# Projections behind two layer ends made block by block, with the norm's transposes between their matmuls, and a third layer that opens with a quarter of z together with the dt columns

## What is computed

```
# layers A and B (A: latent attention, B: attention with forget gates)
hn = rms_norm(h, norm_pre[i])
proj = hn @ w_in[i]                       # values, queries, keys, gates, ...
y = concat(main, mem_out) * silu(gate)
h = h + rms_norm(y @ w_out[i], norm_post[i])
# layer C: a state space branch (SSD) and stick-breaking attention
h = rmsnorm(x, norm_pre)
z_ssd, xbc, dt_raw, q, k, v, z_sb, gates = split(h @ w_in)
xbc = silu(conv(xbc));  dt = softplus(dt_raw + dt_bias)
y = ssd_scan(xs, dt, -exp(a_log), bm, cm, d_skip)    # 16 heads
y_ssd = gated_group_rmsnorm(y, z_ssd) @ w_ssd_proj   # y * silu(z_ssd)
out = (g_ssd * y_ssd + g_sb * y_sb) @ w_out;  x + rmsnorm(out, norm_post)
```

## Time and profile before

| | |
|---|---|
| time, median of 3 | 1274.64 us (1274.6 to 1274.72) |
| time of the profiled execution | 1276.48 us |
| its span, first to last instruction | 1274.7 us |
| PE busy | 1233.7 us (97%) |
| ACT, DVE, POOL busy | 579.5, 530.1, 438.5 us |
| granted TensorE clock, mean | 0.997 |

### The profile page before, as it was taken

The page is one execution under the profiler, slowest core; times in us unless marked ns, Lnnn a source line. Parts: engine busy times, 40 slices in busy tenths (PEclk is TensorE's granted clock), DMA queues, the critical chain, the costliest instruction groups (busy, mean ns, idle before and its releaser), DMA issues. The chain is left out here.

```text
span 1274.7 us, 16603 instructions
## 1 busy us (share of the span) xinstructions
PE 1233.7 (97%) x6339; PEld 947.7 (74%) x6339; DVE 530.1 (42%) x983; ACT 579.5 (45%) x1215; POOL 438.5 (34%) x241
## 2 busy tenths in 40 slices
PE   8999989999999999999899999999999999999998
PEld 7988745578988666678677777778666667878786
DVE  4211655634210455452466445420577771021343
ACT  6354655644333655453544323263555653332242
POOL 5534301213344222213244554343322323444451
PEclk9999989999999999999999999999999999999999
DMA  7433201202235999612223112223211112322331
GB/s 280 133 99 65 66 14 46 67 18 67 79 105 91 72 80 92 84 48 85 67 83 100 50 50 77 72 83 98 68 51 50 51 50 84 98 91 92 99 99 67
DMA packets 111311, 101.01 MB, mean 79 GB/s; under 512 B 22068, under 2 KB 97152, under 8 KB 111232
## 3 DMA queue, kind: packets, MB, share of 16 engines
q1 hardware_dynamic: 108688, 95.35, 31.8%
q0 software_dynamic: 864, 3.15, 0.7%
q10 hardware_dynamic: 1680, 1.44, 0.4%
HBM read 94.68 MB, written 2.10 MB: 76 GB/s over the span
## 5 line engine op out<-in xcount | busy, mean ns | idle before, releaser
L480 POOL TENSOR_TENSOR w_lo<-w_raw,w_hi 128x1024 fp32r<-128x1024 f32 (+4 forms) x172 | 391.7, 2278 | 769.5 <-ACT w_hi L475 769.5
L475 ACT ACTIVATE w_hi<-w_raw 128x1024 fp32r<-128x1024 f32 (+4 forms) x172 | 171.3, 996 | 279.5 <-PE bank L531 237.6
L531 PE MATMUL bank<-acts_hi,w_hi 128*128 128x512 f32 (+1 forms) x600 | 231.8, 386 | 6.4 <-POOL w_lo L480 4.7
L531 PE MATMUL bank<-acts_lo,w_hi 128*128 128x512 f32 (+1 forms) x600 | 230.2, 384 | 0.0
L531 PE MATMUL bank<-acts_hi,w_lo 128*128 128x512 f32 (+1 forms) x600 | 230.2, 384 | 0.0
L531 PEld LDWEIGHTS bank<-acts_hi,w_hi 128*128 128x128 f32 x600 | 112.0, 187 | 32.5 <-issue 5.2
L531 PEld LDWEIGHTS bank<-acts_lo,w_hi 128*128 128x128 f32 x600 | 112.0, 187 | 23.1
L531 PEld LDWEIGHTS bank<-acts_hi,w_lo 128*128 128x128 f32 x600 | 112.0, 187 | 22.3
L531 PE MATMUL bank<-w_hi,acts_hi 128*128 128x512 f32 (+3 forms) x324 | 114.2, 353 | 4.0 <-POOL w_lo L480 1.7
L531 PE MATMUL bank<-w_hi,acts_lo 128*128 128x512 f32 (+3 forms) x324 | 113.5, 350 | 0.0
L531 PE MATMUL bank<-w_lo,acts_hi 128*128 128x512 f32 (+3 forms) x324 | 113.5, 350 | 0.0
(11 more groups left out here) (255 smaller groups left out, 2032.8 us busy)
## 6 DMA issues: line engine op xcount, KB each, us to landing
w_raw<-in_w_in SPq DMA_DIRECT2D x68, 512.0 KB, 3.6
w_raw<-in_w_out SPq DMA_DIRECT2D x24, 512.0 KB, 3.5
w_raw<-in_w_in_b SPq DMA_DIRECT2D x22, 512.0 KB, 4.8
w_raw<-in_w_in_a SPq DMA_DIRECT2D x10, 512.0 KB, 3.8
w_raw<-in_w_mem_kv SPq DMA_DIRECT2D x8, 512.0 KB, 8.0
w_raw<-in_w_sb_proj SPq DMA_DIRECT2D x8, 512.0 KB, 3.4
w_raw<-in_w_ssd_proj SPq DMA_DIRECT2D x8, 512.0 KB, 3.5
w_raw<-in_w_in_b SPq DMA_DIRECT2D x8, 384.0 KB, 3.1
```

The lines of the kernel that those rows point to most:

```text
L475: nc.scalar.activation(w_at(p)[0][:, 0:size], w_raw[p % RAW][:, 0:size], ACT.Copy).then_inc(w_high.sem, 1)
L480: nc.gpsimd.tensor_tensor(lo[:, 0:size], w_raw[p % RAW][:, 0:size], hi[:, 0:size].bitcast(F32), ALU.subtract).then_inc(w_rest.sem, 1)
L531: mm = nc.tensor.matmul(bank_of(S, s, g)[0:lhs.shape[1], 0:rhs.shape[1]], lhs, rhs, start=j + kk + t == 0, stop=j == len(S.pieces) - 1 and ...
```

## The change

Four things change.

1. `pB_v`'s first chunk goes block by block, and turns stand inside projections (`turns_in`): turn 0 after the first piece of block 2 of `pA_out`/`pB_out`, turn 1 after the first piece of its block 3, turns 2 and 3 inside blocks of the projection that follows. The `keep_busy` matmuls at both layer ends are gone. `out_act` rounds four or five pieces ahead instead of two.
2. Layer C opens with `pC_zd`: 256 columns of z and the 16 of dt as one projection of width 272, block by block, four pieces of two rows. `pC_dt` and its transposes are gone. Each of its pieces is fetched by two DMAs (`parts_in`).
3. What is left of z's first half is a chunk of 256 columns. `BESIDE` has more matmuls in slots 0 to 13, and the last slot has 66 instead of 110.
4. `w_more` grows (its start and end, `AR0` and `AR1`, move), two blocks of z stand in `row`, and POOL loads `norm_post` rows later: after all of `pB_v`'s pieces, and after the SSD gates.

```diff
-        pB_v = project(wb, 2 * MAIN_W, 384, 2, MB, tb, to_columns(b_v))
+        pB_v = project(wb, 2 * MAIN_W, 384, 2, MB, tb, to_columns(b_v), by_block=0)
...
-        pC_dt = project(wc, DT0, C_H, 1, 1, by_tokens, lambda S, k, s, g: dtT)
+        ZW = 256
+        pC_zd = project(wc, Z0, ZW + C_H, 1, MB, tb, lambda S, k, s, g: z_left[g][:, 0:ZW], by_block=0,
+                        parts=((Z0, ZW), (DT0, C_H)), rows_each=2)
...
-        pC_z = project(wc, Z0, 512, 2, MB, tb, None)
+        pC_z = project(wc, Z0 + ZW, 512 - ZW, 1, MB, tb, None, rows_each=2)
+        pC_zr = project(wc, Z0 + 512, 512, 1, MB, tb, None)
...
+                    if (block, j) in turns_in:
+                        norm_pe_step(pe, *turns_in[block, j])
...
             for m in range(MB):
                 square(0, m)
+            next_piece(0)
             post_root(0)
             pre_root(0)
             post_root(1)
             rows(0)
             pre_root(1)
             post_root(2)
-            next_piece(0, 4)
+            next_piece(1, 4)
             rows(1)
-            if ahead > 2:
-                next_piece(1, 5)
+            next_piece(2, 5)
             pre_root(2)
-            if ahead > 2:
-                next_piece(2, 6)
             post_root(3)
-            next_piece(*((3, 7) if ahead > 2 else (1, 7)))
+            next_piece(3, 7)
             rows(2)
+            next_piece(4, 6)
             pre_root(3)
             rows(3)
...
-        BESIDE = [3] * (2 * MB) + [4] * C_G + [5, 5] * (C_H + 1) + [6] * (4 * (MB - 1))
+        BESIDE = [6] * (2 * MB) + [8] * C_G + [9, 9, 9, 5] + [5, 5] * (C_H - 1) + [6] * (4 * (MB - 1))
...
-            project_pe(pe, pA_out, ready=attA.low, between_blocks=lambda g: end_blocks(pe, pre[1], g))
-            last_blocks(pe, pre[1], post[0])
-            project_pe(pe, pB_v, pre[1])
+            project_pe(pe, pA_out, ready=attA.low, turns_in={(2, 0): (pre[1], 0), (3, 0): (pre[1], 1)})
+            project_pe(pe, pB_v, pre[1], turns_in={(0, 1): (pre[1], 2), (1, 2): (pre[1], 3)})
...
+            project_pe(pe, pC_zd, pre[2], turns_in={(0, 1): (pre[2], 2), (2, 0): (pre[2], 3)})
+            project_pe(pe, pC_x, also=(sem["ssd_dt"], 1))
```

More of the change, by code:

```diff
@@ L325, in build @@
         off = cut(25088, T)
-        z_left = [cut(at, T) for at in (26112, 26624, 3072, 3584)]
+        z_left = [cut(26112, T), cut(26624, T), row[:, 0:T], row[:, T:D]]
         z_right = c_x[:, :, 0:T]
@@ L371, in project @@
         def project(w, c0, width, n, groups, product, dst, func=ACT.Copy, loop=False, evac=True, first=0,
-                    parity=None, early=0, heads=None, sizes=None, by_block=None):
+                    parity=None, early=0, heads=None, sizes=None, by_block=None, parts=None,
+                    rows_each=None):
             rows = w.shape[0] // P
-            kp = min(rows, PIECE // width)
+            kp = rows_each or min(rows, PIECE // width)
             of_chunk = [(r, min(kp, rows - r)) for r in range(0, rows, kp)]
@@ L452, in heads_in, with parts_in @@
                 sp.dma_start(a, b).then_inc((w_in if x == parts - 1 else w_parts)[p % RAW].sem, 16)
+        def parts_in(sp, S, p, r0, r):
+            to = w_raw[p % RAW][:, 0:r * S.width].rearrange("p (k n) -> p k n", k=r)
+            src, at = S.w.rearrange("(k p) n -> p k n", p=P)[:, r0:r0 + r], 0
+            for c0, n in S.parts:
+                done = w_in if at + n == S.width else w_parts
+                sp.dma_start(to[:, :, at:at + n], src[:, :, c0:c0 + n]).then_inc(done[p % RAW].sem, 16)
+                at += n
         apart = {}
@@ L501, in project_pool, with project_pe @@
             chunk_turns(pool, S, emit)
-        def project_pe(pe, S, acts=None, ready=None, between=None, between_blocks=None):
+        def project_pe(pe, S, acts=None, ready=None, between=None, turns_in=(), also=None):
             if S.banks_free > 0:
@@ L692, in post_stage, with out_act @@
                             root=C["post_root"].take(MB), out=C["post_out"].take(MB), add=C["post_add"].take(MB))
-        def out_act(act, O, S, before, N=None, ahead=4):
+        def out_act(act, O, S, before, N=None):
             def square(half, m):
@@ L1414, in beside_pe @@
                 x_ = (acts_hi, acts_hi, acts_lo)[t]
-                mm = nc.tensor.matmul(bank[ZB + g][:, :], x_[:, 2 * j + kk, g * P:(g + 1) * P],
-                                      w[:, kk * 512:kk * 512 + 512], start=j + kk + t == 0,
+                n = pieces[p][0]
+                mm = nc.tensor.matmul(bank[ZB + g][:, 0:n], x_[:, 2 * j + kk, g * P:(g + 1) * P],
+                                      w[:, kk * n:kk * n + n], start=j + kk + t == 0,
                                       stop=j == 3 and kk == 1 and t == 2)
@@ L1552, in ssd_dve @@
             S = pC_x
-            dve.wait_ge(sem["dt_turned"], 1)
-            link(nc.vector.tensor_tensor(c_u, dt_bank[:, 0:MB * C_H].rearrange("p (m h) -> p m h", m=MB),
-                                         dtb_row.unsqueeze(1).to_broadcast([P, MB, C_H]), ALU.add))
+            for g in range(MB):
+                dve.wait_ge(*pC_zd.evac(g + 1))
+                ins = nc.vector.tensor_tensor(c_u[:, g], bank_of(pC_zd, 0, g)[:, ZW:ZW + C_H], dtb_row, ALU.add)
+            link(ins)
             nc.vector.scalar_tensor_tensor(acs, c_u, -1.0, c_u, ALU.mult, ALU.min).then_inc(sem["ssd_dt"], 1)
@@ L1904, in build @@
             for n in range(2):
-                apart[S.piece0 + 4 + n] = n
-                if S is not pC_out and n == 0:
-                    apart[S.piece0 + 8 + n] = n
+                apart[S.piece0 + 4 + n] = (2 * PIECE * n, PIECE)
+                if S is not pC_out:
+                    apart[S.piece0 + 9 + n] = (2 * PIECE * n, PIECE)
+            if S is not pC_out:
+                apart[S.piece0 + 8] = (4 * PIECE, piece_size(S, 0, 8))
         block = ctx.enter_context(nc.Block())
@@ L1924, in _ @@
             fox_sp(sp)
-            for S in (pB_out, pC_dt, pC_x, pC_z, pC_v, pC_zs):
+            for S in (pB_out, pC_zd, pC_x, pC_z, pC_zr, pC_v, pC_zs):
                 project_sp(sp, S)
@@ L2036, in _ @@
             nc.scalar.preload_act_table_set("sqrt_and_others")
-            out_act(act, post[0], pA_out, latent.sq(2 * MB), pre[1], ahead=2)
-            project_act(act, pB_v)
+            out_act(act, post[0], pA_out, latent.sq(2 * MB), pre[1])
+            project_act(act, pB_v, split=3)
             project_act(act, pB_f)
```

79 lines of the change are left out of this document (32 added, 47 removed).

## The result

| | before | changed |
|---|---|---|
| time, median | 1274.62 us (1273.12 to 1274.72) | 1260.95 us |
| profiled execution | 1276.48 us | 1258.92 us |
| its span | 1274.7 us | 1257.1 us |
| granted TensorE clock, mean | 0.997 | 0.996 |

The ratio is 0.9889, with a 95% interval of 0.9876 to 0.9903: the change is faster by 1.1%. The changed kernel's four executions took 1258.92, 1259.11, 1262.79 and 4205.3 us; why the longest took over three times as long no record shows, it is left out of the ratio, and the median of the other three is 1259.11 us. The forecast was 1256.8 us in a range of 1251.2 to 1262.5.

What follows compares the result with a forecast made beforehand. PE, busy in 97% of the span, was taken as the bound. Terms of -7.1, -4.8, -10.4 and +4.5 us sum to -17.8 us, from a median of 1274.64 to 1256.8 us, range 1251.2 to 1262.5.

Steps and rivals of the forecast that it cites:

- End of layer A: Window behind layer A's projection: 8.3 us go, a wait of about 1.1 us for the fourth weight piece comes; -7.1 us.
- End of layer B: Window behind layer B's projection: 20.2 us go; three turns, `pC_zd` and a 0.8 us wait come back; -4.8 us.
- Head loop: SSD heads: new waits of 6.4 us where weight pieces end in heads' second slots, less 1.9 us before; +4.5 us.
- Slot 13: Head loop: a weight piece ends exactly with this second slot, with a bank to empty; 1.3 us of waits.
- slot 23: Head loop: a weight piece ends two matmuls early in this second slot; 0.5 us of wait.
- slot 33: Head loop, end of z's second chunk: table load and Silus delay `segD[13]` 3.2 us, plus 0.4 for a bank.
- slot 37: Head loop: a weight piece ends exactly with this second slot; 1.0 us of wait.
- the rival of the double price: Head loop: a table switch holds ACT 2.6 us instead of 1.3, two switches; 1259.4 us; chance 0.07.
- The rival of a covered slot 33: Head loop: ACT empties the first three banks early and reaches head 12 in time; 1253.2 us; chance 0.17.
- the late weights: Both layer ends: rounding of pieces two and three slips behind the roots, 3.6 us an end; 1264.0 us; chance 0.12.
- the turns that set the pace: Both layer ends: turns come 3 us or more late, giving back 11.9 us; 1268.7 us; chance 0.04.
- Less of z: Beside work behind layer B's end: 96 matmuls fall from 512 to 256 columns, shortening the last slot; -10.4 us.

## Why the prediction was right

**End of layer A: -7.1, measured -6.9.** The turns were covered, as counted, and the fourth piece was late by 1.03 us for 1.1.

**End of layer B: -4.8, measured -3.5.** The mechanism was right, the wait mis-sized: 1.49 us for 0.8. I had `rest` shrink with its width. POOL's timeline shows two at 544 columns in 4.66 us, 2.3 us each, the fourth piece's first, while DVE was at block 3's sum and `acts_lo` (602.53 to 605.0); one made while DVE was idle took 1.37:

```profile
598.46 1.37 POOL L494 TENSOR_TENSOR w_more<-w_raw,w_more 128x544 fp32r<-128x544 f32 x1 [0.21 <-ACT w_more L489]
602.71 4.66 POOL L494 TENSOR_TENSOR w_lo<-w_raw,w_hi 128x544 fp32r<-128x544 f32 x2 [2.88 <-ACT w_hi L489]
```

Another 0.35 us is `pC_x`, which waits 0.96 us at 633.30 for its own `w_lo`, where the kernel before waited 0.61 us. The other 0.3 us stays open.

**Head loop: +4.5, measured +4.1 in waits.** Slot 13 had 1.3 and cost 0.43 + 0.56; slot 23 0.5 and 0.54; slot 33 3.6 and 0.41 + 3.05; slot 37 1.0 and 1.00: 6.0 us in place of 6.4. ACT's timeline has the order on which slot 33 rests:

```profile
746.45 0.60 ACT L1382 ACTIVATE arena_end<-bank 128x512 f32<-128x512 f32 x1 [3.46 <-PE bank L1485]
747.06 1.28 ACT L1440 ACT_TABLE_LOAD   x1
748.36 2.07 ACT L1440 ACTIVATE arena<-bank 128x512 f32<-128x512 f32 x4
750.28 1.17 ACT L1443 ACTIVATE arena_end<-arena_end 128x512 f32<-128x512 f32 x2
751.32 1.17 ACT L1443 ACTIVATE row<-row 128x512 f32<-128x512 f32 x2
752.36 1.07 ACT L489 ACTIVATE w_hi<-w_raw 128x1024 fp32r<-128x1024 f32 x1
753.45 1.28 ACT L1382 ACT_TABLE_LOAD   x1
754.75 0.60 ACT L1382 ACTIVATE arena_end<-bank 128x512 f32<-128x512 f32 x1
```

Both loads start as the operation ahead ends, and are followed by their first operation 1.30 us after they start. So the rival of the double price is out. By that, the drain that the Trainium skill states (page "ScalarE: Activation LUTs", section "What ACT_TABLE_LOAD costs") does not show in this kernel. The rival of a covered slot 33 is out too (3.05 + 0.41 us of waits), and so are the late weights (1.03 and 1.49 us, not 3.6 more an end) and the turns that set the pace (none waits).

**What the term lacked** is the clock. I priced a wait of 3 us at 3 us; it cost 1.4 more, because PE came out of it at 1.2 GHz. This is the step that was mis-sized.

**Less of z: -10.4.** The stretch fell by 5.1 us; with +4.1 of waits and +1.4 of half clock that leaves -10.6. As the 4.1 counts brackets only, it can be some tenths of a us short. The shorter last slot cost nothing: DVE still idled 9.86 us before its next work (22.96 before).

**The sum, -17.8, met -17.6 between the spans by a balance of things that I had not known of.** The kernel before lost 2.9 us to a half clock at 172, the changed one 1.4 + 1.6 us at 757 and 832. Without them the two executions are 1273.6 and 1255.9 us, 17.7 apart. The median of before holds about 1 us of half clock by this, the 1259.11 of the changed kernel about 3. So the forecast, made from that median, lies 2.3 us under. The terms by themselves were right to 1.3 us each; that their sum met the spans to 0.2 us is luck. The sign that `pC_x` starts near 618 is an instance: it started at 615.84, 2.2 us early, since the execution it was counted from had 2.9 us of half clock ahead of it and the changed one had not. That the half clocks in unprofiled executions cost the same is argued from the mean clocks of the executions (0.999 at 1273.0, 0.998 at 1274.7, 0.997 at 1276.8), not shown.

## What to carry over

A chain that paces PE (scale, turn, scale) is covered by moving useful matmuls between its links; taking out the unused ones alone only turns them into waits, and dearer ones. When an order is packed tighter, write down for each engine what now stands ahead of the operation that the pacing engine asks for next: here one piece fewer on POOL, one root later on ACT and eight Silus later were worth 11 us together, where the change itself was worth some 15. And sum by stretches between the same places of both programs before crediting a total.

## What the hardware showed

**A wait can cost more than its length.** The clock fell to 0.50 near the end of the wait of 3.05 us or just behind it in all three profiles that had it. In the kernel without `keep_busy` it did so at both layer ends, each with two waits of 3.75 to 4.13 us. At the 2.15 us wait it fell in six of the eleven profiles that had it and stayed at 1.00 in five: the same wait to 0.01 us, either way. Near 171, behind a wait of 1.53 us, it fell in three of twelve. It did not fall behind the 1.87 us wait at 614.90 of the kernel before, nor behind that of 1.67 us at 708.28, in three profiles. So below 3 us the length of a wait alone does not decide it. Behind a single wait such a stretch cost 1.4 us (head 13), 1.6 (behind the last slot), and 1.6, 2.8 and 2.9 (near 171). Unused matmuls in the 3.05 us wait kept the clock up in the one profile that had them. One more thing is to be known of the clock rows: they say 1.00 at the very start of the span, where PE comes out of 4.78 us without work, but the `keep_busy` matmuls there (10 in the source, 20 in the trace) took 4.64 us in the kernel before, and the same number at 610.63 took 2.40. By this PE ran at half speed there too, in both kernels alike (4.63 us in the changed one). The half clock is also the likeliest reason, by their mean clocks, that one kernel's executions differ by 1.6, 3.5 or 5 us.

**POOL's time for a piece can depend more on what runs beside it than on its width.** 544 columns took 1.37 us while DVE was idle and 2.05 (at 596.20) and 2.3 us while DVE worked. No experiment changes DVE's work alone, so that DVE is the cause is argued from these rows, not shown.
